# High and low weights of a unit in one buffer, float by float, with the stationary operand read at a step of two

## The reference, cut to what matters

```python
ak_x, av_x, qkv_x, db_x, da_x, aq_x, z_x, gate_x = split_cols(hx @ w_in)
y = jax.nn.sigmoid(g_a) * (attn @ w_pa) + jax.nn.sigmoid(g_d) * (gdn @ w_pd)
return y @ w_out
...
u = dwconv_centred(h @ w_up, conv_w, conv_b)
return (jax.nn.silu(g) * val) @ w_down
...
proj = u @ w_in[l]
h = h + (mix @ w_out[l]).astype(h.dtype)
h = h + jnp.square(jax.nn.relu(z @ w_mlp1[l])) @ w_mlp2[l]
```

## Time and profile before

| | |
|---|---|
| median of 3 runs | 2678.33 us (2673.72 to 2687.87) |
| the profiled execution's own time | 2682.11 us |
| its span | 2680.3 us |
| TensorE matmul (PE) busy | 96% of the span, 19758 instructions |
| weight loads (PEld) busy | 78%, they overlap matmuls |
| VectorE, ScalarE, GpSimd busy | 52%, 38%, 10% |
| mean granted TensorE clock | 0.975 of 2.4 GHz |

### The profile page before, as it was taken

The page is one execution under the profiler, slowest core; times in us unless marked ns, Lnnn a source line. Parts: engine busy times, 40 slices in busy tenths (PEclk is TensorE's granted clock), DMA queues, the critical chain, the costliest instruction groups (busy, mean ns, idle before and its releaser), DMA issues.

```text
span 2680.3 us, 46124 instructions
## 1 busy us (share of the span) xinstructions
PE 2577.4 (96%) x19758; PEld 2081.2 (78%) x19758; DVE 1399.7 (52%) x1950; ACT 1023.4 (38%) x1697; POOL 277.2 (10%) x228
## 2 busy tenths in 40 slices
PE   6998999999998999899999999999999999999998
PEld 5755787778987788688888877788888876788887
DVE  4345698545677433566653546553453446552542
ACT  3245665423334322333333436432233346431222
POOL 0210102223331000111101001100001001100001
PEclk8999999979999999999999989999999999999999
DMA  6100310131003233222323211233232211223322
GB/s 263 57 16 20 114 56 33 65 128 66 4 4 134 86 101 104 101 95 95 98 93 100 87 56 48 79 102 95 95 101 96 87 48 48 95 94 99 98 95 71
DMA packets 64715, 222.91 MB, mean 83 GB/s; under 512 B 7168, under 2 KB 7552, under 8 KB 64384
## 3 DMA queue, kind: packets, MB, share of 16 engines
q1 hardware_dynamic: 63936, 218.39, 24.3%
q10 hardware_dynamic: 576, 1.57, 0.1%
HBM read 213.64 MB, written 6.29 MB: 82 GB/s over the span
## 4 chain that ended last, share of the span: by engine, by line
PE 89%; DVE 6%; issue 2%; ACT 2%; DMA 1%; POOL 0%; SPq 0%; POOLq 0%; DVEq 0%; ACTq 0%
PE ps L321 59%; PE ps L2696 6%; PE ps L1715 5%; PE ps L331 3%; PE ps L837 2%; PE ps L812 1%; PE ps L1721 1%; PE ps L1740 1%; PE ps L1757 1%; DMA ring<-in_w_mod_first 1%; PE ps L2747 1%; DVE w_lo L299 1%; PE ps L828 1%; PE ps L2777 1%; PE ps L1915 1%
## 5 line engine op out<-in xcount | busy, mean ns | idle before, releaser
L299 DVE TENSOR_TENSOR w_lo<-ring,w_hi 128x1024 fp32r<-128x1024 f32 (+1 forms) x339 | 420.7, 1241 | 835.3 <-ACT w_hi L291 835.2
L291 ACT CAST w_hi<-ring 128x1024 fp32r<-128x1024 f32 (+1 forms) x339 | 353.9, 1044 | 922.1 <-PE ps L321 832.2
L321 PE MATMUL ps<-u_hi,w_hi 128*128 128x512 f32 x864 | 338.7, 392 | 9.0 <-DVE u_lo L580 9.0
L321 PE MATMUL ps<-u_hi,w_lo 128*128 128x512 f32 x864 | 336.9, 390 | 0.0
L321 PE MATMUL ps<-u_lo,w_hi 128*128 128x512 f32 x864 | 336.9, 390 | 0.0
L321 PE MATMUL ps<-mid_hi,w_hi 128*128 128x512 f32 x688 | 267.6, 389 | 0.0
L321 PE MATMUL ps<-mid_lo,w_hi 128*128 128x512 f32 x688 | 267.6, 389 | 0.0
L321 PE MATMUL ps<-mid_hi,w_lo 128*128 128x512 f32 x688 | 267.6, 389 | 0.0
L321 PEld LDWEIGHTS ps<-u_hi,w_hi 128*128 128x128 f32 x864 | 162.5, 188 | 46.8 <-issue 8.9
L321 PEld LDWEIGHTS ps<-u_hi,w_lo 128*128 128x128 f32 x864 | 162.6, 188 | 34.0
L321 PEld LDWEIGHTS ps<-u_lo,w_hi 128*128 128x128 f32 x864 | 162.6, 188 | 33.8 <-issue 0.5
(11 more groups left out here) (449 smaller groups left out, 4677.5 us busy)
## 6 DMA issues: line engine op xcount, KB each, us to landing
ring<-in_w_up SPq DMA_DIRECT2D x44, 512.0 KB, 3.4
ring<-in_w_in SPq DMA_DIRECT2D x42, 512.0 KB, 3.5
ring<-in_w_merge SPq DMA_DIRECT2D x32, 512.0 KB, 3.5
ring<-in_w_mlp1a SPq DMA_DIRECT2D x32, 512.0 KB, 3.5
ring<-in_w_mlp2a SPq DMA_DIRECT2D x32, 512.0 KB, 3.5
ring<-in_w_mlp1b SPq DMA_DIRECT2D x32, 512.0 KB, 3.5
ring<-in_w_mlp2b SPq DMA_DIRECT2D x32, 512.0 KB, 3.5
ring<-in_w_gdn_in SPq DMA_DIRECT2D x24, 512.0 KB, 3.5
```

The lines of the kernel that those rows point to most:

```text
L291: nc.scalar.copy(w_hi[:, slot, 0:width], ring[:, n % RING, 0:width]).then_inc(*hi_ok.one())
L299: nc.vector.tensor_tensor(w_lo[:, slot, 0:width], ring[:, n % RING, 0:width], as_f32(w_hi[:, slot, 0:width]), ALU.subtract).then_inc(*lo_o ...
L321: mm = nc.tensor.matmul(dst[:, a:b], w[wi][:, k * P:(k + 1) * P], src[xi][:, k0 + k, a:b], start=start and k == wi == xi == 0, stop=stop a ...
```

## The change

`w_hi` and `w_lo` become one buffer, `w_pair`, of the same total size, with two slots of 2048 floats. A new function, `halves`, says where the two halves of unit n lie. For most units they lie float by float: high, low, high, low, so that each half is an access with a step of two floats (8 bytes). The copy and the subtraction write with this step, the subtraction also reads the high half with it, and TensorE reads its stationary blocks with it. For the units that `rows_of` lists, those that `product_tok` reads as a moving operand (two in `attn_in`, six in each layer's `in2`), the halves lie one after the other as before, each contiguous. `au_half` points to such halves too. No instruction is added or taken away, no wait is changed, and on each of the five engines the instructions stand in the same order as before; only the names and addresses of the operands differ.

```diff
-        w_hi, w_lo = sbr(top, "w_hi", 2, UNIT), sbr(top, "w_lo", 2, UNIT)
+        w_pair = sbr(top, "w_pair", 2, 2 * UNIT)
...
+            by_rows.extend([n in rows_of.get(name, ()) for n in range(len(t_w[name]))])
+
+        rows_of = {"attn_in": range(2), "in2_0": range(3, 9), "in2_1": range(3, 9)}
...
+        def halves(n):
+
+            both = w_pair[:, n_split[n] % 2, :]
+            if by_rows[n]:
+                return both[:, 0:UNIT], both[:, UNIT:2 * UNIT]
+            both = both.rearrange("p (n i) -> p n i", i=2)
+            return both[:, :, 0], both[:, :, 1]
...
-                nc.scalar.copy(w_hi[:, slot, 0:width], ring[:, n % RING, 0:width]).then_inc(*hi_ok.one())
+                nc.scalar.copy(halves(n)[0][:, 0:width], ring[:, n % RING, 0:width]).then_inc(*hi_ok.one())
...
-                nc.vector.tensor_tensor(w_lo[:, slot, 0:width], ring[:, n % RING, 0:width],
-                                        as_f32(w_hi[:, slot, 0:width]), ALU.subtract).then_inc(*lo_ok.one())
+                hi, lo = halves(n)
+                nc.vector.tensor_tensor(lo[:, 0:width], ring[:, n % RING, 0:width], as_f32(hi[:, 0:width]),
+                                        ALU.subtract).then_inc(*lo_ok.one())
...
-            return w_hi[:, n_split[n] % 2, :], w_lo[:, n_split[n] % 2, :]
+            return halves(n)
...
-                    return (w_hi, w_lo)[i][:, g // 2, (g % 2) * QUAD * P:(g % 2 + 1) * QUAD * P]
+                    at_half = i * UNIT + (g % 2) * QUAD * P
+                    return w_pair[:, g // 2, at_half:at_half + QUAD * P]
```

More of the change, by code:

```diff
@@ L225, in build @@
         ident, ones = tab("ident"), tab("ones")
-        units, whole = [], []
+        units, whole, by_rows = [], [], []
         def whole_unit(n):
@@ L282, in ready_to_split @@
                 at[which] += 1
-                yield n, n_split[n] % 2, units[n].shape[1]
+                yield n, units[n].shape[1]
+        def halves(n):
[4 more added lines that the diff above has]
+            return both[:, :, 0], both[:, :, 1]
         def split_hi(act, j):
-            for n, slot, width in ready_to_split("hi", j):
+            for n, width in ready_to_split("hi", j):
                 act.wait_ge(loaded[n % RING], 16 * (n // RING + 1))
@@ L290, in split_hi @@
                     act.wait_ge(unit_used.sem, n - 1)
-                nc.scalar.copy(w_hi[:, slot, 0:width], ring[:, n % RING, 0:width]).then_inc(*hi_ok.one())
+                nc.scalar.copy(halves(n)[0][:, 0:width], ring[:, n % RING, 0:width]).then_inc(*hi_ok.one())
         def split_lo(dve, j):
-            for n, slot, width in ready_to_split("lo", j):
+            for n, width in ready_to_split("lo", j):
                 dve.wait_ge(hi_ok.sem, n_split[n] + 1)
```

## The result

The changed kernel takes 2718.78 us, the median of 4 runs (2714.15 to 2728.76). The kernel before took 2677.55 us beside it, also the median of 4. The ratio is 1.0153, with a 95% interval from 1.0112 to 1.0193: slower by 1.5%, that is by 41 us, and by between 30 and 52 us with the interval. The likeliest case of the prediction, no change, did not come true. The profiled execution of the changed kernel took 2728.76 us, and its granted clock of 0.976 is that of before (0.975), so the clock explains nothing.

The account below looks back on a forecast made before the run. The prediction took the kernel to be bound by TensorE's stream of dense products, at 0.227 us for each 512-column matmul. All its terms were 0, sum 0, so it forecast 2680 us, with a range of 2590 to 2740.

Parts of the forecast that it names:

- The likeliest case of the prediction: Whole kernel: no change, 2680 us, for this case alone 2667 to 2693; chance 0.50.
- rival A: Stationary loads: 1.67 ns a column, 256-column matmuls pay 42 us, uncovered loads some 13, together 2735 us; chance 0.19.
- The stationary read with a step of two, 512 columns: Term for 7752 TensorE matmuls: load pace kept or halved, it stays hidden under the matmul; 0.
- if it takes twice that, 213 ns, it still ends before the 227 ns of the pace are over: 0 again: Bound for loads beside 512-column matmuls: at twice the time per column still 0, with 14 ns to spare.
- A load beside the matmul costs it at most what these rows can show, 0.01 us: Products' last matmuls: VectorE starts 0.43 us after them with or without a load beside, so nothing of 13 ns is seen.
- the prediction's own scale: The 8208 matmuls with stationary weights: one nanosecond on the pace of each is worth 8.2 us, 0.3% of the time.
- Neither is a matter of where the stationary block lies: Each matmul's 13.4 ns over its columns: 10 fixed in float32r, 3 for the step to the next, unaffected by placement; 0.
- 256 columns: Term for 456 matmuls with stationary weights: 0 at unchanged load pace, 42 us at half the load pace; taken as 0.
- Copy and subtraction: ScalarE and VectorE making the halves: subtraction stays 1.24 us, a doubled copy adds 1.05 us each; taken as 0.
- The moving weights: L331 and the delta rule's two matmuls stay contiguous, paces of 0.120 and 0.227 us stay; 0.
- Rival B: Matmuls with stationary weights: 10.4 ns of extra from meeting reads goes away, 85 us gained, 2595 us; chance 0.21.
- Rival C: ScalarE's copy doubles: 12 us where the low half is awaited, as much again if later work is late; to 2704 us; chance 0.10.

Follow-up runs that it names:

- experiment 1: Contiguous writes as before the change, only TensorE's stationary operand read with a step of two: 2719.99 us against 2678.81 for the kernel before, ratio 1.0158.
- experiment 2: Copy and subtraction write with a step of two as in the change, TensorE reads contiguously: 2678.70 us against 2678.81 for the kernel before, ratio 1.0001.
- experiment 7: Contiguous writes, every second unit (slot 0) read with a step of two, the others contiguously: 2703.46 us against 2672.60 for the kernel before.
- experiments 7 and 8: Experiment 7, plus three scans reading units twelve ways in turn (starts, steps, moving starts): 2718.72 us against 2680.12, 2704.43 against 2680.12, 2704.19 against 2691.22.
- experiment 5: Stationary operand read with a step of zero, one float 128 times, contiguous writes: 2700.38 us against 2672.60 for the kernel before.

## Why the prediction went wrong, point by point

The 2719 us lie within the stated range of 2590 to 2740, but that is luck: the range reached so far up for rival A alone, and A's mechanism is not what happened. The sum itself held no term for what was paid.

- **The stationary read with a step of two, 512 columns: "nothing changes: 0".** This is the step that failed. The measured term is +6.6 ns on the long pieces, 42 us at the products and 45 in all, and the read alone brings it (experiment 1), the write alone nothing (experiment 2).
- **The bound "if it takes twice that, 213 ns, it still ends before the 227 ns of the pace are over: 0 again".** This was the fault of reasoning below it. It took a load that ends in time for a load that costs nothing. The load now takes 193 ns and ends in time, and the matmul beside it is slower. With a step of zero the load takes 188, as before, and two matmuls in three are slower too. The slack of the load was never what bounded the price.
- **"A load beside the matmul costs it at most what these rows can show, 0.01 us."** That was read off, and it was too weak a reading in two ways. First, 0.01 us is not small: by the prediction's own scale 6.6 ns on every matmul is 54 us, so a bound of 10 ns excluded nothing. Second, it compared a matmul with a load beside it to one without, while what a load costs is still there one and two matmuls after it (experiment 7); so the matmul without a load was no clean case. The same place in the changed kernel, with no load beside the last matmul:

```profile
1750.33 0.19 PEld L332 LDWEIGHTS ps<-src_hi_buf,w_pair 128*128 128x128 f32 x1
...
1750.56 0.40 PE L332 MATMUL ps<-src_hi_buf,w_pair 128*128 128x512 f32 x1
1750.99 0.69 DVE L2462 TENSOR_TENSOR o_tok<-o_tok,ps 128x512 f32<-128x512 f32 x1 [0.33 <-PE ps L332]
...
1932.98 0.40 PE L332 MATMUL ps<-mid_hi,w_pair 128*128 128x512 f32 x1
1932.99 0.19 PEld L332 LDWEIGHTS ps<-u_hi,w_pair 128*128 128x128 f32 x1
...
1933.42 0.69 DVE L2462 TENSOR_TENSOR o_tok<-o_tok,ps 128x512 f32<-128x512 f32 x1 [3.13 <-PE ps L332]
```

  From the last matmul's start to VectorE's it is 0.43 us without a load beside (1750.56 to 1750.99) and 0.44 with one (1932.98 to 1933.42). In nanoseconds of the trace it is 434 without a load (three such places, 434 and 435), where before it was 426 at all three: the last matmul, with nothing beside it, is slower by 8 ns. With a load it went from 427 to between 432 and 434. So with and without stay alike in both kernels while both have become slower: the comparison could not show the price.
- **"Neither is a matter of where the stationary block lies."** The scans say the opposite: 227 ns for a start at a multiple of 256 bytes, 229 to 234 for the others. Nor does any run show the split of the 13.4 ns into 10 of the type and 3 of the step to the next matmul. It was read off the record's length, and that length moves with the pace at the same type (389 ns before, 394 in the changed kernel).
- **256 columns: 0.** Nearly right: the pairs are at 0.353 us, where before they had 0.347 or 0.354, and a step to or from 256 columns costs 1.2 or 1.3 ns, 1.0 us in all, not 42.
- **Copy and subtraction: 0.** Right in the sum, by experiment 2. The subtraction kept its 1.24 us as VectorE's rows had it; the copy costs 72 ns more, 7%, where the bounds were nothing and double.
- **The moving weights: 0.** Right: 0.120 us for 256 columns, and 227.5 and 227.7 ns for 512.
- **Rival A**, a load that takes twice the time for a column, had the side right and 2735 us is near 2719, but by another mechanism: it wanted a record of 295 ns and 0.44 us for a pair. 193 and 0.353 were measured. It describes a step of four (310 ns, 0.465 us).
- **Rival B**, that two reads meet and a step of two keeps them apart, is refuted as put: 512 columns went up and not down, one float read over and over didn't bring a gain either, and no way of reading had a mean below 226.8 ns. That the two reads have to do with each other is, all the same, what experiments 7 and 8 point to.
- **Rival C** wanted a copy near 2.1 us; it is 1.12.

The rule that the prediction cited, from the Trainium skill, "SBUF — State Buffer", Door 1, the note on cachelines (full bandwidth with at least two accesses to a line of 16 bytes), fits the load's own rate here: 188 and 194 ns with four and two accesses to a line, 310 with one. It doesn't hold the cost of this change, which is on the matmul stream and not on the load's rate.

**What is shown and what stays open.** Shown: the loss is the price of reading the stationary blocks otherwise than contiguously from a 256-byte multiple; with the step of two it is 6 to 7 ns for each float32r matmul of 512 columns, with the other ways of reading that were tried 3 to 9; it begins with the matmul beside the load and lasts for two more; and it takes no step to bring it about. Not shown is what in the buffer or in TensorE makes a start at 256 bytes special. The paces fall near a few values (227, 230 to 231, 233, 235, 238), which would suit two reads that sometimes meet, but the shifts that should then have restored the pace did not, and in experiment 5 the same addresses give 226 ns in one layer and 234 in the other, so the places alone don't decide. Why 256-column matmuls pay so little was not tried apart either.

## What to carry to other kernels

Let the stationary operand of dense float32r matmuls be contiguous and its blocks start at multiples of 256 bytes, and let the moving operand start at such a place too: here every other start or step that was tried cost 1 to 5% of the pace. (On the moving side only starts 4, 8 and 16 bytes late were tried, against multiples of 512, and no step.) It shows in no wait and no share of busy time, only from one start to the next. A load that is hidden can still slow what hides it, so "it ends in time" gives no zero; and where thousands of instructions stand on the path, a reading that is good to 10 ns doesn't bound a price of 7. Ask of a null comparison whether its two cases differ in the thing that the change alters.

## What the runs showed of the hardware that was not expected

- A contiguous stationary block that starts 4 bytes late costs nearly as much as a step of two: 2719.63 us against 2672.60, and 8.5 of the 10.4 us on the long piece. Starts 16, 32, 64 and 128 bytes late have a pace of 233.0 to 233.3 ns, beside 226.8 to 228.2 for a start in place.
- One float late on the moving side makes the pace 238 ns, where 227 is the best.
- The load's record of 188 ns becomes 194, 253 and 310 ns at steps of two, three and four floats, and stays 188 for a step of zero, where all the same two matmuls in three take 232 to 235 ns and the third 226 (long pieces).
- After the last strided load two more matmuls are slow, 232 and 231 ns, before the pace is back at 227, at 112 of 114 passages.
- ScalarE writes 1024 floats at a step of two in 1123 ns against 1051, and VectorE at no extra cost (1246 against 1243).
